# Low halves of the weights in two subtractions of 512 columns, each with its own signal

## What is computed

```python
h = rms_norm(x, norm1_g)
z = h @ w_in                       # 1024 x 9752: short conv, attention, retention, pool, gates
y_a, y_b, y_c, y_d = short_conv_mixer(...), nsa_mixer(...), retention_mixer(...), pool_mixer(...)
gates = sigmoid(z_gate + b_gate)
merged = sum_n(branch_n @ w_branch[n] * gates[n])
x = x + merged @ w_o
h = rms_norm(x, norm2_g)
u_gate, u_val = split(h @ w_up)    # 2 x 2816
x = x + (silu(causal_dwconv(u_gate, ffn_conv)) * u_val) @ w_down
```

## Time and profile before

| | us |
|---|---|
| median of 3 runs | 2175.61 |
| the 3 runs | 2168.34, 2175.61, 2176.33 |
| span of the profiled execution | 2172.4 |
| PE busy | 2098.2 (97%) |
| PEld busy | 1648.3 (76%) |
| DVE busy | 1257.8 (58%) |
| POOL busy | 815.5 (38%) |
| ACT busy | 659.7 (30%) |

### The profile page before, as it was taken

How to read it: one execution, slowest core, us unless ns; L and a number is a source line. 1 busy time by engine, 2 the same in 40 slices (tenths; PEclk the granted TensorE clock), 3 DMA queues, 4 the chain that set the end, 5 groups by cost and what they waited for, 6 DMA issues and landing times.

```text
span 2172.4 us, 31302 instructions
## 1 busy us (share of the span) xinstructions
PE 2098.2 (97%) x9834; PEld 1648.3 (76%) x9834; DVE 1257.8 (58%) x1856; ACT 659.7 (30%) x961; POOL 815.5 (38%) x340
## 2 busy tenths in 40 slices
PE   6999989999999999999999999889999999999997
PEld 5766667788888788888877666667888887888885
DVE  8666776722224888872156668666222278888613
ACT  2244433233332222222223444223332323222222
POOL 3422122344444444435533211233444443444442
PEclk9999999999999999999999999999999999999998
DMA  5311122222222222223232111222222222222322
GB/s 182 106 54 49 42 71 79 78 97 97 97 97 97 89 96 97 97 79 125 97 119 88 55 41 50 68 92 79 97 96 97 97 97 92 96 95 97 105 99 104
DMA packets 57128, 194.86 MB, mean 90 GB/s; under 512 B 6864, under 2 KB 7248, under 8 KB 56912
## 3 DMA queue, kind: packets, MB, share of 16 engines
q1 hardware_dynamic: 52272, 186.14, 25.1%
q10 hardware_dynamic: 4768, 7.61, 1.4%
HBM read 186.64 MB, written 2.10 MB: 87 GB/s over the span
## 4 chain that ended last, share of the span: by engine, by line
issue 70%; POOL 24%; PE 5%; POOLq 1%; DVE 0%; DVEq 0%; ACT 0%
POOL w_lo L413 24%; PE acc L1105 2%; PE acc L1106 2%; PE acc L1107 2%; POOLq L409 0%; POOLq L411 0%; DVE x L1092 0%; DVE rstd L1089 0%; POOLq L413 0%; PE s L1408 0%; DVE x L1079 0%; ACT rstd L583 0%; DVE ssq L1007 0%; DVEq L179 0%; DVE xg_hi L615 0%
## 5 line engine op out<-in xcount | busy, mean ns | idle before, releaser
L413 POOL TENSOR_TENSOR w_lo<-w_raw,w_hi 128x1024 fp32r<-128x1024 f32 x336 | 815.3, 2427 | 1330.6 <-ACT w_hi L429 1319.8
L1105 PE MATMUL acc<-xg_hi,w_hi 128*128 128x512 f32 x1904 | 783.7, 412 | 17.7 <-DVE xg_lo L616 10.5
L1107 PE MATMUL acc<-xg_hi,w_lo 128*128 128x512 f32 x1904 | 750.1, 394 | 0.0
L1106 PE MATMUL acc<-xg_lo,w_hi 128*128 128x512 f32 x1904 | 749.2, 394 | 0.0
L429 ACT ACTIVATE w_hi<-w_raw 128x1024 fp32r<-128x1024 f32 x336 | 355.0, 1057 | 897.2 <-PE acc L1107 826.0
L1105 PEld LDWEIGHTS acc<-xg_hi,w_hi 128*128 128x128 f32 x1904 | 362.3, 190 | 130.9 <-issue 46.2
L1106 PEld LDWEIGHTS acc<-xg_lo,w_hi 128*128 128x128 f32 x1904 | 363.0, 191 | 76.7 <-issue 7.3
L1107 PEld LDWEIGHTS acc<-xg_hi,w_lo 128*128 128x128 f32 x1904 | 361.8, 190 | 78.1
L985 DVE TENSOR_TENSOR work<-acc,rstd 128x512 f32<-128x512 f32 x64 | 44.1, 690 | 254.7 <-PE acc L1107 254.5
L1105 PE MATMUL acc<-act_hi,w_hi 128*128 128x512 f32 x352 | 137.2, 390 | 0.4 <-POOL w_lo L413 0.4
L1107 PE MATMUL acc<-act_hi,w_lo 128*128 128x512 f32 x352 | 137.0, 389 | 0.0
(11 more groups left out here) (190 smaller groups left out, 2205.5 us busy)
## 6 DMA issues: line engine op xcount, KB each, us to landing
w_raw<-weights_dram SPq DMA_DIRECT2D x339, 512.0 KB, 3.2
x<-xT_dram SPq DMA_DIRECT2D x8, 256.0 KB, 5.3
rot<-rq ACTq DMA_DIRECT2D x16, 128.0 KB
rot<-rk ACTq DMA_DIRECT2D x16, 128.0 KB
dec<-decay_dram ACTq DMA_DIRECT2D x8, 256.0 KB, 4.0
out_dram<-x SPq DMA_DIRECT2D x8, 256.0 KB, 2.2
con<-consts_dram SPq DMA_DIRECT2D x1, 1598.0 KB, 9.9
w1k<-w_dram SPq DMA_DIRECT2D x2, 512.0 KB, 9.3
```

The costliest lines, as they stand in the source:

```text
L413: nc.gpsimd.tensor_tensor(w_lo[:, k, :], w_raw[:, k, :], w_hi[:, k, :].bitcast(F32), ALU.subtract).then_inc(lo_ready, 1)
L1105: mm(tile, w_h, right_hi, start=first, stop=False)
L1106: mm(tile, w_h, right_lo, start=False, stop=False)
L1107: return mm(tile, w_l, right_hi, start=False, stop=last)
```

## The change

POOL makes the low half of a group in two subtractions of 512 columns, and each raises `lo_ready` by one, so that a group raises it by two. TensorE waits at the first chunk of a group for the first of the two, and at its fifth chunk for the second (`second_half`, new). In stage B the fifth chunk is the head of the third `quarter`, behind the small matmuls that stand between the second and the third. In J's branch products the second of the two tiles of a group is the one that waits, in O and D the chunk in the middle. SP's waits count by two, and ask for both halves of the group that held the slot, as before. The total of columns, the loads, and the work of ACT and DVE stay as they are.

```diff
-                        sp.wait_ge(lo_ready, 1 + g - (RING - 1))
+                        sp.wait_ge(lo_ready, 1 + 2 * (g - (RING - 1)))
...
-                    nc.gpsimd.tensor_tensor(w_lo[:, k, :], w_raw[:, k, :], w_hi[:, k, :].bitcast(F32),
-                                            ALU.subtract).then_inc(lo_ready, 1)
+                    for half in range(2):
+                        part = slice(half * CH * P // 2, (half + 1) * CH * P // 2)
+                        nc.gpsimd.tensor_tensor(w_lo[:, k, part], w_raw[:, k, part], w_hi[:, k, part].bitcast(F32),
+                                                ALU.subtract).then_inc(lo_ready, 1)
...
                     pe.wait_ge(hi_ready, v)
-                    pe.wait_ge(lo_ready, 1 + v)
+                    pe.wait_ge(lo_ready, 2 * v)
+
+                def second_half(g, loop=None, per=0):
+
+                    v = L * GROUPS + (g + 1)
+                    if loop is not None:
+                        v = v + loop * per
+                    pe.wait_ge(lo_ready, 1 + 2 * v)
...
-                def quarter(g, q, tile, wait=False):
-
+                def quarter(g, q, tile, wait=False, loop=None, per=0):
+
+                    if q == 2:
+                        second_half(g, loop, per)
                     for c in (2 * q, 2 * q + 1):
...
+                        if n % 2:
+                            second_half(g, j, J_GROUPS)
                         for c in range(BC):
...
+                        if c == DC // 2:
+                            second_half(g)
                         ins = product(acc[T % 2][:, :], g % RING, c, mrg_hi[:, c, :], mrg_lo[:, c, :], c == 0, c == DC - 1)
...
+                            if c % CH == CH // 2:
+                                second_half(g, t, 2 * DG)
```

More of the change, by code:

```diff
@@ L387, in _ @@
                     g = RING + k
-                    sp.wait_ge(lo_ready, 1 + L * GROUPS + (g - (RING - 1)))
+                    sp.wait_ge(lo_ready, 1 + 2 * (L * GROUPS + (g - (RING - 1))))
                     load_group(L * GROUPS + g, g % RING)
@@ L1134, in quarter, with projection @@
                         ins.then_inc(halves, 1)
-                def projection(g, tile, wait=False, norm=None):
+                def projection(g, tile, wait=False, norm=None, loop=None, per=0):
                     for q in range(4):
-                        quarter(g, q, tile, wait)
+                        quarter(g, q, tile, wait, loop, per)
                         if norm and q == 2:
@@ L1350, in _ @@
                         tile_free(TJ0 + n, j, 8)
-                        projection(J0 + n, acc[n % 2])
+                        projection(J0 + n, acc[n % 2], loop=j, per=J_GROUPS)
                     for n in range(4):
@@ L1386, in _ @@
                         tile_free(TU0 + 2 + k, t, 6)
-                        projection(U0 + 2 + k, acc[k % 2])
+                        projection(U0 + 2 + k, acc[k % 2], loop=t, per=6)
                 with pe.Fori(0, DC // 2) as t:
```

## The result

The changed kernel takes 2154.28 us (median of four runs, 2152.31 to 2154.99) and the kernel before 2174.36 (2168.34 to 2176.33). The ratio is 0.9917, with a 95% interval of 0.9899 to 0.9934: 20 us off, where 5.6 were forecast. The profiled execution has a span of 2150.5 us and a mean granted clock of 0.988, beside 2172.4 us and 0.984 before.

What follows compares the result with a forecast made beforehand. TensorE's own rate bounds J, O, U and D; in B it waits at small steps. Terms 3.0 + 1.0 + 1.0 + 0.5 + 0.6 - 0.5 = 5.6 us off 2175.6 gave 2170.0 us, range 2160 to 2181.

Steps and rivals of the forecast that it cites:

- turns: POOL and DVE alternate: a single held operation gains up to 1.2 us, a chain of two or more 0.1 to 0.2.
- The clock: Behind the `rk` waits in B: a shorter wait leaves the clock up once, 1.0 us gained (between 0 and 3.4).
- moved-up order at `rk`: Before `ret_scores`: DVE's first operation gets in before POOL's first half, 1.4 us gained at two of four places, 0.1 elsewhere.
- chains of five and more: Two `rk` waits (chain of five), kernel start and window sums (six to eight on SBUF): 0 gained.
- cmp_p behind L971: Single held DVE operation freed 1.1 us sooner, uncovering the softmax's first step: about 0.5 us twice, 1.0 us gained.
- end of B: L933 held with L935 behind it: 0.1 us if turns stay, 0.4 if L933 comes first; together 0.5 us gained.
- start of D: The fourth group is loaded late and TensorE starts on its first half: 0.3 us, twice, 0.6 us gained.
- register operations: Some 170 added on TensorE in attention stages: zero in J to D, 0.5 us lost in B, 15 if all show.
- POOL's half: Each subtraction of 512 columns takes 1.25 us, 2.50 a group; 34 us more POOL work, none on the path.
- The rival that DVE wins both halves: Queued DVE operations go ahead of POOL's second half, each chain gains 1.2 us: 13 to 15 us, 2161; chance 0.14.
- mid-tile waits: 336 waits added on matmuls in the middle of groups: forecast free; a rival had 50 ns each, 2187 us, chance 0.12 with register operations.
- the third rival: Queued DVE operations go ahead of POOL's second half, including 2 us of clock: 13 to 15 us, 2161; chance 0.14.

Runs made afterwards that it cites:

- the two runs by stage: Kernel before, one signal, two subtractions per group in only the first 45 groups of each layer: 2158.90 us; in only the other 123: 2170.94 us.
- the waits alone: Kernel before with one subtraction and one signal, plus the change's 336 mid-group waits and register operations on TensorE: 2172.80 us, ratio 0.9996.
- two pieces in the rest: Kernel before, one signal, two subtractions per group only in the last 123 groups of each layer: 2170.94 us, ratio 0.9987.
- two in A and B: Kernel before, one signal, two subtractions per group only in the first 45 groups of each layer: 2158.90 us, ratio 0.9928.

## Why the prediction missed

The direction and the mechanism (turns, half a hold) were right, and the size was off by a factor of more than three: 2170.0 was forecast with a range from 2160, and 2154.3 came. Three steps of the sum failed. The clock was put at 1.0 us, and it gave some 5. The moved-up order at `rk` was given to two of four places, 3.0 us, and it came at all four, 5.4 us. And chains of five and more were put at nothing, and the places behind them gave 2.5 us; the start of the kernel gave 3.3 more, which is luck. The terms of the sum, with what the matmul-by-matmul comparison of the two traces shows (us gained, both layers together):

```
term                                             forecast   measured
rk of the second and third wait, four places        3.0       5.4
rk of the first wait, two places (chain of five)    0        -0.5
rv_T in front of it, two places                     0         2.2
cmp_p behind L971 (waits 3.3 -> 2.4)                1.0       0.9
end of B, two places                                0.5       1.1
start of D, two places                              0.6       0.7
window sums (97.8 and 1166.9 us), two places        0         0.8
kT at 44.7 us                                       0         1.1
start of the kernel                                 0         2.2
register operations                                -0.5       0
clock                                               1.0       3.5 to 6.5
```

- *POOL's half.* 1.25 us taken, 1.29 measured. With all sizes that were run (204, 460, 740, 1290 and 2396 ns where nothing disturbs it, for 8, 128, 256, 512 and 1024 columns) a subtraction is 0.18 us and 2.16 ns for each column. The Trainium skill's figure ("GPSIMD Engine Reference", section "Performance versus the Vector engine") had led to an estimate of 1.35 and a fixed part of 0.3; the measurement decides.
- *Turns.* Right: L1035 and the timeline show them. The rival that DVE wins both halves is out, although its time of 2161 was the nearest: that was luck.
- *Who comes first at `rk`.* I gave the moved-up order to two of four places. It came at all four, with 1.34 to 1.37 us each beside the 1.4 that I had worked out. The mechanism was right, and the count was too careful.
- *"The other two waits follow a chain of five: 0", "start of the kernel and the window sums: chains of six to eight on SBUF: 0".* The first is wrong by 1.7 us, the second by 0.8 us at the window sums. A turn costs a chain a whole half only while POOL has halves left to do, and POOL has two for each group. So a long chain outlasts them. Some of its members also have no need of POOL's leave. The RECIPROCAL between the rotation and the transposition of `rv` is one (L895 takes 1.74 us beside a subtraction, and L893 1.74 without one), and so in front of `rv_T` stands a single held operation, then one that runs beside POOL. The changed kernel, then the kernel before:

```profile
306.32 1.73 POOL L415 TENSOR_TENSOR w_lo<-w_raw,w_hi 128x512 fp32r<-128x512 f32 x1
306.84 1.74 DVE L895 RECIPROCAL pT<-pT 128x256 f32<-128x256 f32 x1
308.70 0.69 DVE L650 TENSOR_TENSOR rv_T<-acc,rstd 128x512 f32<-128x512 f32 x1
...
309.63 0.63 PE L1191 MATMUL t<-con,rv_T 128*128 128x128 f32 x4 [0.53 <-DVE rv_T L650]
```

```profile
312.23 2.40 POOL L413 TENSOR_TENSOR w_lo<-w_raw,w_hi 128x1024 fp32r<-128x1024 f32 x1 [6.73 <-ACT w_hi L429]
313.25 1.92 DVE L692 TENSOR_TENSOR rq<-rq,rot 128x512 f32<-128x512 f32 x1
...
317.89 0.63 PE L1180 MATMUL t<-con,rv_T 128*128 128x128 f32 x4 [1.65 <-DVE rv_T L648]
```

  L692 was held 1.23 us by the whole subtraction, and its counterpart by 0.12 (0.81 us at 306.10). TensorE's wait for `rv_T` went from 1.65 to 0.53 us. The waits for `rk` right behind did grow by 0.2 to 0.26 us each. All runs with two equal halves in A and B show the 0.90 to 0.94 us from matmul to matmul at both `rv_T` places, beside 2.03 and 2.04 before.

  The start of the kernel is another matter. The 2.2 us there came since the next subtraction missed the chain in this execution (see the two runs by stage above), and the 1.1 us of `kT` aren't the cut's: the step is 1.34 us before, but 0.25 with the waits alone and with two pieces in the rest, where A isn't cut, and 1.22 with two in A and B. Over the first 108 us the changed kernel leads by 1.4 us only, as its clock is lower there (0.91 against 0.94 in the first 54). To have this chain at 0 was a fair guess, and 3.3 of the 13.9 us of waits are luck.
- *The mid-tile waits* cost nothing and gained nothing, as said. *J to D* stayed at 240 matmuls, as said. *The start of D* gained 0.3 us a layer, as said. The prediction has no gaps between 430 and 1087 us, which isn't so at the turn from O to U: 229 matmuls in the 54 us from 702 before, and 229 from 700 now. Nothing hung on it.
- *The clock.* Over 23 runs of the kernel before the mean granted clock is 0.9842, over the four of the changed kernel 0.9870. As (1 - clock) times the time that is 34.4 us against 28.0, 6.4 less. A line through 35 runs of unchanged chains (these 23 and the twelve with the waits alone) gives 18.5 us for 0.01 of clock, which makes it 5.2. Against another 16 runs of the kernel before, with a mean of 0.9851, it would be 3.5. I had allowed 1.0, one stretch. That stretch is there: behind the second of the four waits the clock is 0.51 in the earlier trace rows and 1.00 in the row of 377.95 above, where TensorE had stood still for 1.94 us instead of 3.3. The prediction says that the clock fell behind three of the six waits for `rk`; in its trace it fell behind four, as a low stretch begins at 1458.2 us as well. But low stretches come behind many small waits, at some 13 places before and nine after, and which of them fall low differs between executions of one kernel. The run of the waits alone, whose chains are those of the kernel before, had a profiled execution of 2162.0 us at 0.989, and 2178.2 as its slowest run at 0.983. Its profiled execution leads that of the kernel before by 10.5 us at the end, although the medians are the same. So the lead of one execution can be read for single waits, and not for the clock. The split of the 20 us is 13 to 14 for waits (12.9 by time times clock) and some 5 for the clock, between 3.5 and 6.5. How the latter is shared among places, and whether shorter waits are its whole cause, stays open.
- *The range.* Its lower end was the third rival, worked out with 2 us of clock. Three errors of the same sign (four places and not two, chains called zero, the clock) and the luck at the start of the kernel added up, and the range had held no term for that.

The Trainium skill ("SBUF — State Buffer", section "Who interferes with whom") says that whoever of VectorE and GpSimd issues first keeps the shared ports for its whole instruction. The holds of 2.15 ns for each column of the piece agree, but for some 0.14 us of GpSimd's instruction that hold nobody. What the runs add is that a held VectorE instruction waits for one GpSimd instruction at most, so that the length of that one is the price.

## To carry over

Where two engines exclude each other instruction by instruction, as POOL and DVE do here, let the engine off the critical path work in short instructions, even if that makes it busier: POOL went from 815 to 1321 us of work here, and the kernel from 2174 to 2133. Cut until the fixed part of a piece begins to make the result late (at eight pieces one wait of 1.7 us had come; more weren't tried), and cut equally, since a chain meets the longest piece. Before calling the gain for a chain zero, count how many pieces are queued against how many of its instructions need the port, and sum the small places too: nearly twenty of 0.3 to 1.4 us and one of 3 us made up this gain, and the clock, which falls behind such waits, gave some 5 us on top. And look at the same place in several runs before calling its gain the change's: the one of 3 us was there in some runs with equal halves and not in others.

## What had not been expected of the hardware

- A subtraction on GpSimd takes 2.16 ns a column and 0.18 us. The longest holds of VectorE, 0.32 to 2.20 us for 128 to 1024 columns, are 2.10 ns a column and 0.04 us. So most of the fixed part holds nobody: cutting costs GpSimd 0.18 us a piece, and VectorE gains. Its holds were 277 us with one piece and 54 with eight.
- With eight pieces only 152 instructions of 1856 are held by over 0.15 us, where four have 386. One piece holds for 0.3 us at most there, and an instruction that meets it partway falls under that mark; whether that is all of it stays open.
- GpSimd's subtractions cost this kernel up to 53 us, 2.4% of its time, although the list of waits names GpSimd for 0.4 us only the earlier trace rows. It shows nowhere but in the length of VectorE's instructions: an operation of one size with two durations, such as 0.69 and 2.84 us in the earlier trace rows, is its sign.
